# The attention mixer of a two-part network on one NeuronCore: local attention's units put between the pieces of a projection, stick-breaking attention in rounds of one head, masked on TensorE

## The reference, cut to what matters

```
qa, ka, va, qb, kb, vb = jnp.split((h @ w_in).astype(f32), cuts, axis=-1)
qa = rope(rms_norm(qa.reshape(B, S, SWA_HEADS, HEAD_DIM), q_norm), positions)
ka = rope(rms_norm(ka.reshape(B, S, SWA_KV_HEADS, HEAD_DIM), k_norm), positions)
out_a = sliding_window_attention(qa, ka, va, sinks)
out_b = stick_breaking_attention(heads_b(qb), heads_b(kb), heads_b(vb))
return jnp.concatenate([out_a, out_b], axis=-1).astype(h.dtype) @ w_out
```

```
z = jnp.einsum('bqhd,bkhd->bhqk', q[:, t0:t1], k[:, :t1]) * (HEAD_DIM ** -0.5)
log_fail = jnp.where(causal, -jax.nn.softplus(z), 0.0)
log_after = lax.cumsum(log_fail, axis=3, reverse=True) - log_fail
a = jnp.where(causal, jnp.exp(jax.nn.log_sigmoid(z) + log_after), 0.0)
outs.append(jnp.einsum('bhqk,bkhd->bqhd', a, v[:, :t1]))
```

## Time and profile before

| what | value |
|---|---|
| median of 3 runs (lowest to highest) | 4330.69 us (4327.8 to 4332.04) |
| profiled execution: time, span | 4329.3 us, 4327.5 us |
| PE, DVE, ACT, POOL busy | 91%, 49%, 37%, 14% |
| mean granted TensorE clock | 0.937 |
| vb's projection | 2566.3 to 2588.2 us |
| local attention's units | 2591.6 to 2661.9 us |
| stick-breaking heads | 2661.9 to 2773.0 us |
| transposes, then the output projection begins | 2773.0 to 2778.9 us |

### The profile page before, as it was taken

One profiled execution on the slowest core, in us unless ns is written; L12 is line 12 of the kernel. 1 busy time (PEld: TensorE's weight loads), 2 busy tenths in 40 slices (PEclk: granted clock), 3 DMA queues, 4 the chain that ended last, 5 costly groups with the idle time before them and its releaser, 6 DMA issues.

```text
span 4327.5 us, 67031 instructions
## 1 busy us (share of the span) xinstructions
PE 3916.8 (91%) x28034; PEld 3240.4 (75%) x28034; DVE 2124.9 (49%) x3061; ACT 1587.7 (37%) x2550; POOL 588.5 (14%) x692
## 2 busy tenths in 40 slices
PE   6988897878999988988899798898999998889999
PEld 4866786766888766856788586677888787677887
DVE  3545554656121453277423656454555427545564
ACT  3333333333111332164323334544334336544333
POOL 0035303532000001002100000200120003000220
PEclk8988898888999999999899895999999999899999
DMA  4234433131111121103122320141323230322322
GB/s 153 81 129 145 143 95 116 35 106 56 62 63 65 54 80 59 59 1 109 59 98 93 73 93 1 33 136 40 97 95 102 83 112 17 102 86 69 98 98 88
DMA packets 248532, 355.04 MB, mean 82 GB/s; under 512 B 9299, under 2 KB 158502, under 8 KB 247846
## 3 DMA queue, kind: packets, MB, share of 16 engines
q1 hardware_dynamic: 233840, 300.49, 21.5%
q0 software_dynamic: 13840, 50.11, 3.7%
q10 hardware_dynamic: 550, 0.17, 0.0%
HBM read 336.50 MB, written 14.24 MB: 81 GB/s over the span
## 4 chain that ended last, share of the span: by engine, by line
PE 77%; DVE 11%; ACT 6%; POOL 2%; issue 2%; DMA 1%; ACTq 0%; DVEq 0%; SPq 0%; POOLq 0%
PE psum L233 20%; PE psum L235 20%; PE psum L234 20%; PE psum L230 13%; ACT arena L341 3%; PE psum L239 3%; DVE arena L264 3%; DVE arena L274 2%; DVE rx L335 2%; POOL arena L379 1%; DVE rw L264 1%; DVE arena L278 1%; ACT arena L345 1%; ACT rw L345 1%; DVE arena L270 1%
## 5 line engine op out<-in xcount | busy, mean ns | idle before, releaser
L233 PE MATMUL psum<-rx,rw 128*128 128x512 f32 (+2 forms) x2768 | 1026.3, 371 | 47.0 <-DVE rx L335 29.1
L234 PE MATMUL psum<-rx,rw 128*128 128x512 f32 (+2 forms) x2768 | 1011.1, 365 | 0.0
L235 PE MATMUL psum<-rx,rw 128*128 128x512 f32 (+2 forms) x2768 | 1010.4, 365 | 0.0
L230 PE MATMUL psum<-arena 32*32 32x32 f32 (+10 forms) x13078 | 833.3, 260 | 173.7 <-ACT arena L345 59.7
L264 DVE TENSOR_TENSOR rw<-arena,rw 128x2048 fp32r<-128x2048 f32 (+2 forms) x239 | 538.5, 2253 | 862.5 <-ACT rw L345 857.4
L230 PEld LDWEIGHTS psum<-arena 32*32 32x32 f32 (+5 forms) x13078 | 649.1, 144 | 339.0 <-issue 108.4
L345 ACT ACTIVATE rw<-arena 128x2048 fp32r<-128x2048 f32 (+2 forms) x239 | 448.2, 1875 | 802.5 <-PE psum L235 780.6
L233 PE MATMUL psum<-rw,rx 128*128 128x512 f32 (+1 forms) x1720 | 676.7, 393 | 36.8 <-DVE rx L335 27.6
L234 PE MATMUL psum<-rw,rx 128*128 128x512 f32 (+1 forms) x1720 | 670.5, 390 | 0.0
L235 PE MATMUL psum<-rw,rx 128*128 128x512 f32 (+1 forms) x1720 | 670.3, 390 | 0.0
L233 PEld LDWEIGHTS psum<-rx,rw 128*128 128x128 f32 (+1 forms) x2768 | 530.8, 192 | 144.9 <-DVE rx L335 41.3
(11 more groups left out here) (71 smaller groups left out, 2068.7 us busy)
## 6 DMA issues: line engine op xcount, KB each, us to landing
arena<-in_ffn_w_up SPq DMA_DIRECT2D x66, 1024.0 KB, 5.1
...
```

Source lines behind the costliest of these rows:

```text
L230: return self.e.matmul(out, l, r, start=start, stop=stop)
L233: self.e.matmul(out, l[0], r[0], start=start, stop=False)
L234: self.e.matmul(out, l[0], r[1], start=False, stop=False)
L235: return self.e.matmul(out, l[1], r[0], start=False, stop=stop)
```

## The change

- PE no longer waits for `ab_ksw` behind vb but ahead of it: the 6 transposes come between kb and vb. Behind each of vb's 8 pieces stand two steps of local attention (`pe_sw`): the scores of unit i, the product of unit i-2, the transposes of unit i-1. Two last steps follow head 0's scores of stick-breaking attention.
- The masks of both attentions are added in PSUM, by a matmul of the identity with a mask, both fp32r (made by 9 small ACT copies at the stage's start). In a local unit DVE then takes the maximum from PSUM, and ACT applies factor, bias and exponential and adds up the row, for each head of the pair apart. POOL's two mask steps in each stick-breaking head are gone, as are the four mask and subtraction steps over wide tiles of DVE.
- Stick-breaking attention runs in 11 rounds: in round i PE does "after" of head i-1, the product of head i-2, the transposes of one block of local attention's result (rounds 1 to 4), and the scores of head i+1. The scores and the "after" of a head take 3 banks, not 4, and DVE 3 instructions, not 4. qb gets its factor 0.125 in ACT's copy out of PSUM.
- The product is turned round: vb's 64 columns are the weights and a's up to 512 columns stream, 4 matmuls for a head, with features down the partitions, so that 4 of the 8 blocks need no transposes and no copy.
- The meetings are gone. POOL begins its loads for the next layer when the last block is done.
- On DVE the casts of kb's second tile and of vb's first stand behind the fourth rotation and the copy of swapped k; ACT's square roots stand ahead of its copies of qb.

```diff
-    c[:, C_US:C_US + 128] = p < f
+    c[:, C_US:C_US + 128] = np.where(p < f, 0, -BIG)
...
+            elif t == tiles[-1]:
+                ins.then_inc(*p.sig(("used", m)))
+            if behind:
+                behind(kh, t)
...
-    pe_proj_tok(p, K, "ab_vb", wi[:, 1792:2304], K.H5, t4)
     p.wait_ge(*K.at("ab_ksw"))
...
+    def behind(kh, t):
+        for i in (kh * 8 + t * 2, kh * 8 + t * 2 + 1):
+            pe_sw(p, K, i)
+    pe_proj_tok(p, K, "ab_vb", wi[:, 1792:2304], K.H5, t4, None, behind)
+    sb_scores(p, K, 0)
+    for i in (16, 17):
+        pe_sw(p, K, i)
...
+    us = cs[:, 256:384]
+    for dst, src in zip(sw_mask(K), (K.ident, cs[:, 0:256])):
+        a.cp(dst, src).then_inc(*a.sig("sw_mask"))
+    for o, by in ((0, 1.0), (128, 0.0), (256, 0.0), (384, 1.0), (512, 0.0), (640, 0.0), (768, 0.0)):
+        a.cp(K.rx[:, 8576 + o:8704 + o], us, scale=by).then_inc(*a.sig("sb_mask"))
...
-    for tag, dst, t0 in (("ab_qb", qb5, 0), ("ab_kb", kb5, 2)):
-        for j in range(2):
+    for f in range(4):
+        if f % 2 == 0:
             a.tile()
-            for f in (2 * j, 2 * j + 1):
-                a.wait_ge(*K.at(tag, f, 0))
-                a.cp(dst[:, f, :], K.ps(tag, f, 0)[:, :]).then_inc(*a.sig())
-                a.free(tag, f, 0)
...
+        a.root(K.tmpc[:, 60:70], ("ab", f))
+        feat("ab_qb", qb5, f, 0.125)
+    for f in range(4):
+        if f % 2 == 0:
+            a.tile()
+        feat("ab_kb", kb5, f, 1.0)
...
     for t in range(4):
-        v.tile()
+        if t % 2 == 0:
+            v.tile()
         dve_rotate(v, K, t)
-    v.tile()
-    v.tile()
     ksw = swapped_k(K)
     v.cp(ksw[:, :, 0:64], qk[:, :, 576:640]).then_inc(*v.sig())
     v.cp(ksw[:, :, 64:128], qk[:, :, 512:576]).then_inc(*v.sig("ab_ksw"))
+    v.tile()
+    v.tile()
     for k in range(1, 6, 2):
         v.wait_ge(*K.at("ab_T", k))
-        v.cp(q5[:, k, :] if k < 4 else k5[:, k - 4, :], K.ps("ab_T", k)[:, :]).then_inc(*v.sig())
+        v.cp(q5[:, k, :] if k < 4 else k5[:, k - 4, :], K.ps("ab_T", k)[:, :]).then_inc(*v.sig("ab_T_d"))
...
+    for i in range(18):
+        if i in (0, 8):
+            v.tile()
+        dve_sw(v, K, i)
...
+            kT, pr = k5[:, 0 if h // 4 == half else 1, :], slice(half * 64, half * 64 + 64)
+            p.mm(b[:, u * size:(u + 1) * size], q5[pr, h // 2, blk * 128:(blk + 1) * 128],
+                 kT[pr, (blk + 1) * 128 - size:(blk + 1) * 128], True, False)
+            ins = p.mm(b[:, u * size:(u + 1) * size], one, mask[:, 256 - size:256], False, True)
+        ins.then_inc(*p.sig(("sw_s", i)))
+        p.close("sw_s", i)
...
+    if sw_unit(i - 2):
+        blk, hp = sw_unit(i - 2)
+        pt, nb = sw_mem(K, i - 2)[1], sw_size(i - 2) // 128
+        p.wait_ge(*K.at("sw_p", i - 2))
...
+    if sw_unit(i - 1):
+        e = sw_mem(K, i - 1)[0]
+        p.wait_ge(*K.at("sw_e", i - 1))
...
+        a.wait_ge(*K.at("sw_d", i))
+        if i >= 4:
+            a.wait_ge(*K.at("sw_T", i - 4))
+        for u in range(2):
+            a.act(e[:, u * size:(u + 1) * size], K.ps("sw_s", i)[:, u * size:(u + 1) * size], ACT.Exp, scale=0.125,
+                  bias=bias[:, u:u + 1], accum_out=total[:, u:u + 1]).then_inc(*a.sig(("sw_e", i)))
+        a.free("sw_s", i)
+        a.act(sink, sink, ACT.Exp).then_inc(*a.sig(("sw_sum", i)))
...
+        v.red(bias, r2(K.ps("sw_s", i)[:, 0:2 * sw_size(i)], 2), MAX).then_inc(*v.sig())
+        v.stt(bias, bias, -0.125, sinks(K)[:, hp:hp + 3:2], MUL, MIN).then_inc(*v.sig())
+        v.tt(sink, snk[:, hp:hp + 3:2], bias, ADD).then_inc(*v.sig(("sw_d", i)))
...
+SB_COL = {0: 0, 1: 512, 3: 896, 2: 1024}
+SB_BANKS = [(1, 3), (2,), (0,)]
...
+    for j, kbs in enumerate(SB_BANKS):
+        b, c = p.bank("sb_z", h, j), sb_part(j)
+        p.mm(b[:, 0:c.stop - c.start], sw_mask(K)[0], sb_mask(K, j), True, False)
+        for kb in kbs:
+            o, n = SB_COL[kb] - SB_COL[kbs[0]], sb_size(kb)
+            ins = p.mm(b[:, o:o + n], kb5[pr, h // 2, kb * 128:kb * 128 + 128], qb5[pr, h // 2, kb * 128:512], False,
+                       kb == kbs[-1])
...
+        ins = p.mm(b[pr, kb * 128:512], vb[:, kb, h * 64:h * 64 + 64], a[:, SB_COL[kb]:SB_COL[kb] + n], kb == 0, kb == 3)
...
+def pe_sb(p, K):
+    sb_scores(p, K, 1)
+    for i in SB_ROUNDS:
+        if 0 <= i - 1 < 8:
+            sb_after(p, K, i - 1)
+        if 0 <= i - 2 < 8:
+            sb_product(p, K, i - 2)
+        if 1 <= i < 5:
+            pe_ab_turn(p, K, i - 1)
+        if 2 <= i + 1 < 8:
+            sb_scores(p, K, i + 1)
...
+def act_sb(a, K):
+    for i in SB_ROUNDS:
+        for k in sb_blocks(i):
+            act_ab_hi(a, K, k)
+        if i < 8:
+            z, s = sb_mem(K, i)
+            if i >= 2:
+                a.wait_ge(*K.at("sb_after", i - 2, 2))
+            a.wait_ge(*K.at("sb_zs", i))
+            a.act(s, z, ACT.Abs).then_inc(*a.sig())
+            a.act(s, s, ACT.Exp, scale=-1.0).then_inc(*a.sig())
+            a.act(s, s, ACT.Ln, bias=1.0).then_inc(*a.sig(("sb_ln", i)))
+        if 0 <= i - 1 < 8:
+            z = sb_mem(K, i - 1)[0]
+            a.wait_ge(*K.at("sb_loga", i - 1))
+            a.act(z, z, ACT.Exp).then_inc(*a.sig(("sb_a", i - 1)))
...
+def dve_sb(v, K):
+    dve_zs(v, K, 0)
+    for i in SB_ROUNDS:
+        for k in sb_blocks(i):
+            dve_ab_lo(v, K, k)
+        if 0 <= i - 1 < 8:
+            z = sb_mem(K, i - 1)[0]
+            for j in range(3):
+                c = sb_part(j)
+                v.wait_ge(*K.at("sb_after", i - 1, j))
+                v.tt(z[:, c], z[:, c], sb_bank(K, "sb_after", i - 1, j), SUB).then_inc(*v.sig(("sb_loga", i - 1)))
+                v.free("sb_after", i - 1, j)
+        if i < 8:
+            z, s = sb_mem(K, i)
+            v.wait_ge(*K.at("sb_ln", i))
+            v.stt(s, z, 0.0, s, MAX, ADD).then_inc(*v.sig(("sb_sp", i)))
+        if i + 1 < 8:
+            dve_zs(v, K, i + 1)
...
-    g.meet("ab_proj")
-    g.meet("sw")
-    pipeline([pool_sb_unit(g, K, h) for h in range(8)], 2)
-    g.meet("sb")
+    g.wait_ge(*K.at("abT", 7))
```

More of the change, by code:

```diff
@@ L713, in pe_proj_feat, with pe_proj_tok @@
                 p.close(*key)
-def pe_proj_tok(p, K, tag, src, hT, tiles, ready=None):
+            if behind:
+                behind(c0 // 128 + f)
+def pe_proj_tok(p, K, tag, src, hT, tiles, ready=None, behind=None):
     n = src.shape[1]
@@ L2719, with sw_size, pe_sw @@
-CB = [(0, 512), (512, 384), (896, 256), (1152, 128)]
-def sb_mem(K, h):
-    o = SWW + 416 + h % 2 * 2560
-    return K.mem(o, 1280), K.mem(o + 1280, 1280)
-def pe_sb_unit(p, K, h):
+    c = K.tmpc[:, j * 8:j * 8 + 8]
+    return K.mem(SWW + 1600 + j * 1024, 512), K.mem(SWW + 2112 + j * 1024, 512), c[:, 0:2], c[:, 2:4], c[:, 4:6]
+def sw_size(n):
+    return 256 if SW_UNITS[n][0] else 128
+def pe_sw(p, K, i):
+    qk, q5, k5, va, qb5, kb5, vb = ab_mem(K)
+    one, mask = sw_mask(K)
+    if sw_unit(i):
+        blk, hp = sw_unit(i)
+        size = sw_size(i)
+        if i == 0:
+            p.wait_ge(*K.at("sw_mask"))
+            p.wait_ge(*K.at("ab_T_a"))
+            p.wait_ge(*K.at("ab_T_d"))
+        b = p.bank("sw_s", i)
+        for u in range(2):
+            h = hp + 2 * u
+            half = h % 2
+            kT, pr = k5[:, 0 if h // 4 == half else 1, :], slice(half * 64, half * 64 + 64)
[8 more added lines that the diff above has]
+        p.wait_ge(*K.at("sw_p", i - 2))
+        b = p.bank("sw_o", i - 2)
+        for u in range(2):
+            g = (hp + 2 * u) // 4
+            for k in range(nb):
+                ins = p.mm(b[:, u * 64:u * 64 + 64], pt[:, (u * nb + k) * 128:(u * nb + k + 1) * 128],
+                           va[:, blk - nb + 1 + k, g * 64:g * 64 + 64], k == 0, k == nb - 1)
+        ins.then_inc(*p.sig(("sw_o", i - 2)))
+        p.close("sw_o", i - 2)
+    if sw_unit(i - 1):
+        e = sw_mem(K, i - 1)[0]
+        p.wait_ge(*K.at("sw_e", i - 1))
+        b = p.bank("sw_T", i - 1)
+        for q in range(2 * sw_size(i - 1) // 128):
+            ins = p.tr(b[:, q * 128:(q + 1) * 128], e[:, q * 128:(q + 1) * 128])
+        ins.then_inc(*p.sig(("sw_T", i - 1)))
+        p.close("sw_T", i - 1)
@@ new lines, with sb_size, sb_part, sb_mask @@
+SB_COL = {0: 0, 1: 512, 3: 896, 2: 1024}
+SB_BANKS = [(1, 3), (2,), (0,)]
+SB_ROUNDS = range(11)
+def sb_size(kb):
+    return 512 - 128 * kb
+def sb_part(j):
+    o = SB_COL[SB_BANKS[j][0]]
+    return slice(o, o + sum(sb_size(kb) for kb in SB_BANKS[j]))
+def sb_mask(K, j):
+    o, n = ((8576, 512), (8960, 256), (8960, 512))[j]
+    return K.rx[:, o:o + n]
+def sb_mem(K, h):
+    return K.mem(SWW + (6960, 416, 4256, 5536)[h % 4], 1280), K.mem(SWW + (1696, 2976)[h % 2], 1280)
+def sb_bank(K, tag, h, j):
+    c = sb_part(j)
+    return K.ps(tag, h, j)[:, 0:c.stop - c.start]
@@ new lines, in sb_product @@
+def sb_product(p, K, h):
+    vb, a = ab_mem(K)[6], sb_mem(K, h)[0]
+    k, pr = 4 + h // 2, slice(h % 2 * 64, h % 2 * 64 + 64)
+    if h == 0:
+        p.wait_ge(*K.at("ab_vb_out"))
```

(32 more changed lines are left out.)

286 lines of the change are left out of this document (93 added, 193 removed).

## The result

| | us |
|---|---|
| before, median | 4330.69 |
| after, median of 5 (lowest to highest) | 4301.46 (4296.69 to 4314.93) |
| ratio, 95% interval | 0.9938 (0.9919 to 0.9957) |
| predicted (range) | 4286 (4268 to 4316) |

What follows compares the result with a forecast made beforehand. It took the 190.7 us from vb's end to the output projection, PE waiting or at low clock, as the bound; terms moved that projection from 2778.9 to 2731.8, 47.1 saved, less 2.5: 44.6, so 4286 us (4268 to 4316).

Steps and rivals of the forecast that it cites:

- Casts behind the rotations: At kb's second tile: PE waits 6.8 us for DVE's late cast; with other losses, 9.2 us late together.
- the half clock behind the pause: After PE's wait at kb's second tile: about 3.5 us at half clock, 1.9 us lost.
- Clock between the pieces: Local units between vb's dense pieces: clock 1.00 in most 5 us stretches; units take 35.8 us, not 70.3.
- The rival of half clock in some pairs: Vb with local units: half clock in half of the pairs, +24 us, 4310 us; chance 0.10.
- took off 2.5: Local units: 2.5 us taken off the saving for a piece at half clock behind the first pair's wait.
- Two masks of 256 columns at the fp32r rate, 0.23: Local unit on PE: its two mask matmuls cost 0.23 us of the unit's 2.55.
- 1280 mask columns, 0.57: Stick-breaking scores of a head on PE: masks cost 0.57 us at the fp32r rate, within 2.74.
- masks at the fp32 rate: Mask matmuls in both attentions run at the fp32 rate: +21 us, 4307 us; chance 0.07.
- To head 0's "after": Way into stick-breaking attention: scores 2.74, wait 0.7, then 9.0 us through DVE and ACT, reached at 2658.2.
- The waits of a pair: Second step of each local pair: PE waits about 1.0 us for ACT's copy, in 7 pairs.
- The waits at the casts: First local pair: vb's second-tile casts stand ahead of unit 0's steps; PE finishes scores some 3.0 us early.
- Rounds and tail: Stick-breaking attention, PE the bound: round 1 10.0 us, rounds 2 to 6 47.5, tail 16.1.

Runs made afterwards that it cites:

- e_cast: Changed kernel with kb's second tile cast between third and fourth rotation, vb's first behind the fourth, ACT's casts moved alike: 4294.0 us, ratio to before 0.9907.
- e_seq: Changed kernel with all eight vb pieces run first, then the 16 local units in the new form, nothing between: 4329.3 us, ratio to before 0.9998.
- e_fp32mask: Changed kernel with identity and mask as fp32 operands in the local units alone, in place of fp32r copies: 4303.7 us.

## Why the prediction was right, and where its size was off

**Casts behind the rotations: right.** PE waited 6.5 us (forecast 6.8); ab_T begins 63.0 us behind the mark, forecast 63.0 (2575.5 less 2512.56). Undone, it gave back 8.8, so the half clock behind the pause cost 2.3 (forecast 1.9). One thing is wrong in what I wrote under "The change": the cast that stood between the third and fourth rotation was vb's first; kb's second stood between the second and third, at 2550.95, and the sum used that time. So e_cast put it in a place of its own, one rotation later than before.

**Clock between the pieces: right in kind.** It is 1.00 in most of the units' time, where the old units stood at 0.54, and e_seq shows that the pieces do it. The rival of half clock in some pairs came true in a small part: 6.8 us, where I took off 2.5. Each low stretch in the units begins in a wait of PE or within 1.7 us behind one, but not each wait brings one: in the changed kernel the clock falls at the waits of 1.07 and 0.59 us (2589.56 and 2599.42), not at that of 1.46 (2630.79).

**"Two masks of 256 columns at the fp32r rate, 0.23", "1280 mask columns, 0.57": the terms that were mis-sized.** The columns' rate was right, but each mask stands between matmuls of 64 rows, and each change exposes some 0.2 us. In the local part the sum had 3.8 us for masks (12 x 0.23, 4 x 0.12 and head 0's 0.57); on PE they cost 13.2. In a round they cost 1.55 (10.75 less 9.2), not 0.57. So the sum was 9.4 us short by them in the local part and some 5 in rounds 2 to 6. The rival "masks at the fp32 rate" (+21) comes near that with the wrong mechanism: masks in fp32 would have added to the changes (e_fp32mask).

**To head 0's "after"** the sum with its 2.5 was 148.1 behind the mark; it was 159.5, so 11.4 more. To the last transposes I had 62.1 us of PE's work and 10.0 of waits. It was 74.0 (9.4 more by masks, 2.5 by pieces of 2.95 us, not 2.74, and the rest of a unit), 4.3 of waits and 6.8 by the clock: 11.9 - 5.7 + 4.3 = 10.5. From there it was 11.5 for 10.6. The waits of a pair were 0.3 to 0.6, not 1.0, since the scores that cover them were longer than forecast; with cheaper masks they grew to 0.5 and more. So part of the masks' price was hidden by waits that I had counted and that didn't come (5.7 us): that much of the nearness of the sum is luck. The waits at the casts I had seen for the first pair (3.0; it was 1.1) and not for the second tile (1.5).

**Rounds and tail** took 82.2 us for 73.6. Rounds 2 to 6, with three turned blocks, took 54.9 for 47.5; 5 x 1.0 of that are masks; of the 0.5 a round that are left (a round without masks is 9.2, forecast 8.67) "after" and product are 0.33 (4.53 and 2.30 us for 4.33 and 2.17), the rest the change from scores to "after", which stands there without masks too. The first was 10.7 for 10.0, the tail 16.6 for 16.1. PE was the bound as forecast: busy 81.4 of 82.1 us, ACT 60.3; ACT's table loads held up no round. The 11.4 and 8.6 us together are the 20.0 by which the mixer's saving (24.6) fell short of 44.6; that the medians fell short by 15.4 only is that drift, and luck.
